# Token-major projection blocks as quads of 512-column passes

## The reference

```python
h = rms_norm(x, norm1_w[layer])
(q, k_c, v_c, k_s, v_s, k_w, v_w, g_nsa, z, xbc, dt_raw,
 gate_a, gate_b) = split_columns(h @ w_in[layer], IN_SIZES)
y_a = nsa_mixer(q, k_c, v_c, k_s, v_s, k_w, v_w, g_nsa, ...)   # 4 groups of 4 heads
y_b = ssd_mixer(z, xbc, dt_raw, ...)                           # 4 groups of 8 heads
merged = jax.nn.sigmoid(gate_a) * (y_a @ w_proj_a[layer]) + jax.nn.sigmoid(gate_b) * (y_b @ w_proj_b[layer])
x = x + merged @ w_out[layer]
x = x + conv_glu_ffn(rms_norm(x, norm2_w[layer]), ...)
```

## Time and profile before

| | |
|---|---|
| runs (median, lowest, highest) | 1243.16, 1242.79, 1243.5 us |
| span of the profiled execution | 1241.6 us |
| its own time outside the span | not given; the median lies 1.56 us above the span |
| TensorE busy in the span | 1229.4 us |
| VectorE busy | 843.6 us |
| ScalarE busy | 635.3 us |
| group stage | about 110 to 655 us, some 136.5 us for a group |

### The profile page before, as it was taken

How to read it: one execution, slowest core, us unless ns; L and a number is a source line. 1 busy time by engine, 2 the same in 40 slices (tenths; PEclk the granted TensorE clock), 3 DMA queues, 4 the chain that set the end, 5 groups by cost and what they waited for, 6 DMA issues and landing times.

```text
span 1241.6 us, 17772 instructions
## 1 busy us (share of the span) xinstructions
PE 1229.4 (99%) x6725; PEld 1054.2 (85%) x6725; DVE 843.6 (68%) x1611; ACT 635.3 (51%) x1201; POOL 88.3 (7%) x78
## 2 busy tenths in 40 slices
PE   7999999999999999999999999999999999999998
PEld 6998998899978998888978888888888888888887
DVE  4526988898879887899774643333788888884221
ACT  6616777678775868676775633223423222332110
POOL 1000001400042001400040000000000000000000
PEclk9999999999999999999999999999999999999999
DMA  8512321132212221132116623335233333334341
GB/s 243 162 34 66 86 60 47 48 105 63 63 44 74 80 67 54 51 102 61 54 40 219 222 86 93 93 97 179 64 102 96 91 102 102 88 101 136 102 128 42
DMA packets 185737, 116.34 MB, mean 94 GB/s; under 512 B 25933, under 2 KB 169909, under 8 KB 185653
## 3 DMA queue, kind: packets, MB, share of 16 engines
q1 hardware_dynamic: 182023, 108.86, 30.5%
q10 hardware_dynamic: 3630, 6.35, 1.4%
HBM read 106.80 MB, written 8.39 MB: 93 GB/s over the span
## 4 chain that ended last, share of the span: by engine, by line
PE 94%; DVE 3%; ACT 1%; issue 1%; ACTq 0%; DVEq 0%
PE g L609 16%; PE g L611 16%; PE g L610 16%; PE t L602 5%; PE g L650 5%; PE g L652 5%; PE g L651 5%; PE ob L800 3%; PE s L784 3%; PE s L959 2%; PE s L960 2%; PE s L958 2%; PE t L706 1%; PE s L881 1%; PE g L959 1%; PE g L958 1%
## 5 line engine op out<-in xcount | busy, mean ns | idle before, releaser
L1027 ACT ACTIVATE w_high<-wraw 128x1024 fp32r<-128x1024 f32 x175 | 185.2, 1059 | 279.6 <-DMA wraw<-in_ffn_w_up 135.6
L1551 DVE TENSOR_TENSOR w_low<-wraw,w_high 128x1024 fp32r<-128x1024 f32 x174 | 216.7, 1248 | 125.7 <-ACT w_high L1027 123.2
L609 PE MATMUL g<-hT_hi,w_high 128*128 128x512 f32 x360 | 158.3, 440 | 1.2 <-DVE hT_lo L1557 1.2
L650 PE MATMUL g<-w_high,hT_hi 128*128 128x256 f32 x512 | 151.7, 296 | 0.2 <-DVE w_low L1551 0.2
L652 PE MATMUL g<-w_high,hT_lo 128*128 128x256 f32 x512 | 144.7, 283 | 0.0
L651 PE MATMUL g<-w_low,hT_hi 128*128 128x256 f32 x512 | 144.6, 282 | 0.0
L611 PE MATMUL g<-hT_hi,w_low 128*128 128x512 f32 x360 | 141.1, 392 | 0.0
L610 PE MATMUL g<-hT_lo,w_high 128*128 128x512 f32 x360 | 140.9, 391 | 0.0
L609 PE MATMUL g<-h2T_hi,w_high 128*128 128x512 f32 x352 | 137.4, 390 | 0.1
L610 PE MATMUL g<-h2T_lo,w_high 128*128 128x512 f32 x352 | 137.0, 389 | 0.0
L611 PE MATMUL g<-h2T_hi,w_low 128*128 128x512 f32 x352 | 137.0, 389 | 0.0
(11 more groups left out here) (348 smaller groups left out, 2528.4 us busy)
## 6 DMA issues: line engine op xcount, KB each, us to landing
wraw<-in_w_in SPq DMA_DIRECT2D x152, 256.0 KB, 3.3
wraw<-in_ffn_w_up SPq DMA_DIRECT2D x88, 256.0 KB, 3.3
wraw<-in_ffn_w_down SPq DMA_DIRECT2D x44, 256.0 KB, 3.3
wraw<-in_w_proj_b SPq DMA_DIRECT2D x32, 256.0 KB, 3.2
yT_lo<-spill SPq DMA_DIRECT2D x6, 1024.0 KB, 10.4
spill<-piece_e ACTq DMA_DIRECT2D x16, 256.0 KB, 4.4
wraw<-in_w_proj_a SPq DMA_DIRECT2D x16, 256.0 KB, 3.2
wraw<-in_w_out SPq DMA_DIRECT2D x16, 256.0 KB, 3.3
```

What stands on the lines that cost most here:

```text
L609: nc.tensor.matmul(gb[par][:, :], w, hi, start=k == 0, stop=False)
L650: nc.tensor.matmul(out_, hT[0][:, k, cols], w, start=k == 0, stop=False)
L1027: nc.scalar.activation(whi[slot_of(u)][:, :, :], wraw[u % 2][:, :, :], ACT.Copy).then_inc(w_hi, 1)
L1551: V.tensor_tensor(wlo[slot_of(u)][:, :, :], wraw[u % 2][:, :, :], whi[slot_of(u)][:, :, :].bitcast(F32), ALU.subtract).then_inc(w_lo, 1)
```

## The change

The 28 token-major blocks become seven *quads* of four blocks: one for q, k, v in each of the first three groups, one for z in each of the four. A unit of a quad is no longer 1024 rows by 128 columns but 256 rows (two row tiles) by 512 columns; the four units q = 0 to 3 together are the 1024x512 weight. A block is the 128x512 result of one token tile i. Window n of a quad runs four of the sixteen pairs (i, q), two passes of 512 columns deep: 24 passes. Windows 0 and 1 fill the banks of tiles 0 and 1, windows 2 and 3 those of tiles 2 and 3; a tile is finished in its second window. Both windows of a half use both banks. In the second window of a quad the order is (0,2), (1,2), (0,3), (1,3); in the others a tile's two pairs follow each other. A window waits for a unit's low part only where tile 0 first uses it.

Around it: the raw loads of q, k, v have runs of 1 KB and 256 B where they had 512 B or 256 B; slots of a quad's units 0 and 1 come free in its third window, those of units 2 and 3 at its end; ScalarE copies tiles out in odd windows only, the first of the two after `exps` and ahead of `pT_hi` of tile 2; the `hi` calls stand at the ends of the iterations by a table; the C block is copied out ahead of the last y tile in groups 1 to 3; VectorE's `lo` in iterations 2 and 6 moves behind the convolution, so just ahead of `scale` of the next one.

```diff
+            def quad_window(u, n, between):
+                first, half = u - n, n % 2
+                a, b = (0, 1) if n < 2 else (2, 3)
+                c, d = 2 * half, 2 * half + 1
+                order = ((a, c), (b, c), (a, d), (b, d)) if n == 1 else ((a, c), (a, d), (b, c), (b, d))
+                for place, (i, q) in enumerate(order):
+                    if half == 0 and q == 0:
+                        pe.wait_ge(g_rel, first + i - 1)
+                    if i == 0:
+                        pe.wait_ge(w_lo, first + q + 1)
+                    w, wl = wide(whi[slot_of(first + q)]), wide(wlo[slot_of(first + q)])
+                    for kk in range(2):
+                        if 2 * place + kk in between:
+                            between[2 * place + kk]()
+                        h, l = (t[:, 2 * q + kk, P * i:P * (i + 1)] for t in hT)
+                        out_ = gb[(first + i) % 2][:, :]
+                        nc.tensor.matmul(out_, h, w[:, kk, :], start=q == 0 and kk == 0, stop=False)
+                        nc.tensor.matmul(out_, h, wl[:, kk, :], start=False, stop=False)
+                        ins = nc.tensor.matmul(out_, l, w[:, kk, :], start=False, stop=q == 3 and kk == 1)
+                    if q == 3:
+                        ins.then_inc(mm_done, 1)
+                    if n == 2 and i == 3:
+                        ins.then_inc(quad_rows, 1)
...
-                    if u in PAIRS or u - 1 in PAIRS:
-                        half_pair(u, n % 2, between)
+                    if n >= 4 or g < G - 1:
+                        quad_window(u, n % 4, between)
...
+                ROUND_END = {0: (3,), 2: (4, 5), 3: (6,), 4: (7,), 6: (8, 9), 7: (10,)}
...
+                def evac_heads(i):
+                    u = u0 + OQ + i
                     act.wait_ge(mm_done, u + 1)
+                    src = gb[u % 2][:, :].rearrange("p (b n) -> p b n", b=4)
+                    nc.scalar.activation(tokq[:, :, i, :], src, ACT.Copy)
+                    nc.scalar.activation(sq[:, :, i, :], src[:, 0:2, :], ACT.Square)
+                    nc.scalar.activation(sq_k[:, :, i, :], src[:, 2:4, 0:DH], ACT.Square).then_inc(g_rel, 1)
...
                         if 0 < n < 7 and j == 1:
                             exps(n + 1, (3, 2))
                         if n == 0 and j == 1:
-                            evac_x(g, 5)
+                            if g:
+                                hi(u0 + OQ + 2)
+                            else:
+                                evac_x(g, 5)
+                        if n % 2 and j == 1:
+                            evac_tile(n, 0)
...
-                    evac_mid(n)
+                    if n < 4 and g == G - 1:
+                        evac_block(n)
+                    elif n % 2:
+                        evac_tile(n, 1)
+                    for q in ROUND_END.get(n, ()):
+                        hi(u0 + OQ + q)
...
-                    lo(u0 + 4 + n)
+                    if n not in (2, 6):
+                        lo(u0 + 4 + n)
...
                     if n > 1:
                         conv(g, CONVS[n - 2])
+                    if n in (2, 6):
+                        lo(u0 + 4 + n)
```

More of the change, by code:

```diff
@@ L72, with last_in_slot, loads_to, blocks_done @@
 X0_UNITS = (7, 10, 11, 12)
-PAIRS = {5, 8} | {U_GRP + GROUP_BLOCKS * g + o for g in range(G) for o in ((OQ, OQ + 2, OZ, OZ + 2) if g < G - 1 else (OZ, OZ + 2))}
+PAIRS = {5, 8}
+QUADS = [U_GRP + GROUP_BLOCKS * g + o for g in range(G) for o in (OQ, OZ) if g < G - 1 or o == OZ]
 def slot_of(u):
     return (u if u < PRE_BLOCKS else u + 1) % SLOTS
-def done_for_slot(u):
+def last_in_slot(u):
     before = [v for v in range(u) if slot_of(v) == slot_of(u)]
-    if not before:
-        return 0
-    return before[-1] + (2 if before[-1] in PAIRS else 1)
+    return before[-1] if before else None
+def loads_to(u):
+    heads = [first + q for first in QUADS if (first - U_GRP) % GROUP_BLOCKS == OQ for q in range(4)]
+    return sum(48 if v in heads else 32 for v in range(u % 2, u + 1, 2))
+def blocks_done(v):
+    for first in QUADS:
+        if first + 2 <= v < first + 4:
+            return first + 4
+    return v + (2 if v in PAIRS else 1)
+def quad_rows_over(v):
+    for k, first in enumerate(QUADS):
+        if first <= v < first + 2:
+            return 2 * k + v - first + 1
+    return 0
 class Count:
@@ L424, in qkv, with wide_load, heads_rows, z_rows @@
                 sides(u, w_in_cols(g * DH + k, DH), DH, w_in_cols(g * DH + v, DH), DH)
+            def wide_load(u, w, kq, h):
+                v = w[2 * P * kq:2 * P * (kq + 1), D // 2 * h:D // 2 * (h + 1)].rearrange("(k p) n -> p k n", p=P)
+                load(u, [(wide(wraw[u % 2])[:, kk, :], v[:, kk, :]) for kk in range(2)])
+            def heads_rows(u, g, q):
+                rows = slice(2 * P * q, 2 * P * (q + 1))
+                dst = wide(wraw[u % 2])
+                qw = io["w_in"][0, rows, C_Q + 256 * g:C_Q + 256 * (g + 1)]
+                kv = io["w_in"][0, rows, C_KS:C_KS + 4 * 256].rearrange("(k p) (s n) -> p k s n", p=P, s=4)
+                load(u, [(dst[:, :, 0:256], qw.rearrange("(k p) n -> p k n", p=P))] + [
+                    (dst[:, kk, 256:512].rearrange("p (s n) -> p s n", s=4), kv[:, kk, :, DH * g:DH * (g + 1)])
+                    for kk in range(2)])
+            def z_rows(u, g, q):
+                wide_load(u, io["w_in"][0, :, C_Z + 512 * g:C_Z + 512 * (g + 1)], q, 0)
             def x_in(u, g, q):
@@ L446, in _ @@
                     if g < G - 1:
-                        qkv(u0 + OQ + b, g + 1, b)
+                        heads_rows(u0 + OQ + b, g + 1, b)
                     else:
@@ L480, in _ @@
                     halves(m * 3 + (U_MRG + q), w[:, m * P:(m + 1) * P])
-            def wide_load(u, w, kq, h):
-                v = w[2 * P * kq:2 * P * (kq + 1), D // 2 * h:D // 2 * (h + 1)].rearrange("(k p) n -> p k n", p=P)
-                load(u, [(wide(wraw[u % 2])[:, kk, :], v[:, kk, :]) for kk in range(2)])
             def out_unit(q):
@@ L1022, in hi @@
             def hi(u):
-                if done_for_slot(u):
-                    act.wait_ge(mm_done, done_for_slot(u))
-                act.wait_ge(w_loaded[u % 2], 32 * (u // 2 + 1))
+                v = last_in_slot(u)
+                if v is not None:
+                    if quad_rows_over(v):
+                        act.wait_ge(quad_rows, quad_rows_over(v))
+                    else:
+                        act.wait_ge(mm_done, blocks_done(v))
+                act.wait_ge(w_loaded[u % 2], loads_to(u))
                 nc.scalar.activation(whi[slot_of(u)][:, :, :], wraw[u % 2][:, :, :], ACT.Copy).then_inc(w_hi, 1)
@@ L1181, in y_scale, with y_back_out @@
                     nc.scalar.activation(zs[:, c, :], zs[:, c, :], ACT.Copy, scale=rstd[:, c:c + 1]).then_inc(yn_ready, 1)
-            def y_back_out(g):
+            def y_back_out(g, before_last=None):
                 act.wait_ge(t_rel, tau_of(g + 1, K_Y))
                 for b in range(4):
+                    if b == 3 and before_last:
+                        before_last()
                     tau = tau_of(g + 1, K_Y + b)
@@ L1214, in evac_gate, with evac_z, evac_tile, evac_block @@
                     hi(u + 3)
-                def evac_z(n):
-                    u, h, half = u0 + OQ + n, n % 2, n // 2 - 2
+                def evac_heads(i):
+                    u = u0 + OQ + i
                     act.wait_ge(mm_done, u + 1)
[L1220 to L1224, removed]
+                    src = gb[u % 2][:, :].rearrange("p (b n) -> p b n", b=4)
+                    nc.scalar.activation(tokq[:, :, i, :], src, ACT.Copy)
+                    nc.scalar.activation(sq[:, :, i, :], src[:, 0:2, :], ACT.Square)
+                    nc.scalar.activation(sq_k[:, :, i, :], src[:, 2:4, 0:DH], ACT.Square).then_inc(g_rel, 1)
+                def evac_z(c):
+                    u = u0 + OZ + c
+                    act.wait_ge(mm_done, u + 1)
+                    nc.scalar.activation(zs[:, c, :], gb[u % 2][:, :], ACT.Copy).then_inc(g_rel, 1)
+                def evac_tile(n, i):
+                    if n >= 4:
+                        evac_z(2 * (n // 2 - 2) + i)
+                    elif g < G - 1:
+                        if n == 1 and i == 0:
+                            act.wait_ge(v_lo, g * 2 + 2)
+                        evac_heads(2 * (n // 2) + i)
+                def evac_block(n):
                     if n == 0:
                         act.wait_ge(v_lo, g * 2 + 2)
[L1228 to L1233, removed]
+                    u = u0 + OQ + n
+                    act.wait_ge(mm_done, u + 1)
+                    nc.scalar.activation(gate_tile(n), gb[u % 2][:, :], ACT.Copy).then_inc(g_rel, 1)
                 def evac_late(q):
```

8 lines of the change are left out of this document (5 added, 3 removed).

## The result

The changed kernel takes 1247.75 us (median of 5 runs, 1247.24 to 1248.54) against 1243.17 us before (1242.79 to 1243.5), a ratio of 1.0036 with a 95% interval of 1.0023 to 1.0049. Forecast were 1246.4 us, slower, with an own range of 1244.5 to 1249.5. The span of the profiled execution grew from 1241.6 to 1246.8 us; that execution took 1248.54 us and was the slowest of the five, 0.8 us above the median, so the trace shows a little more than the 4.6 us between the medians.

The account below looks back on a forecast made before the run. TensorE was taken as the bound, with VectorE close to it. Window 1's 3.7, window 3's 2.4 and window 5's 0.4 less 3.3 saved by passes gave +3.2 us, 1246.4 us by median, range 1244.5 to 1249.5.

Parts of the forecast that it names:

- the two links of window 1: TensorE waits for a late low part at step 4, then for ScalarE's copy ahead of `cs`; 3.7 us in all.
- the signs I had named: Passes at 0.227 to 0.232 us, gaps in windows 1 and 3, group 1's z quad half a microsecond shorter.
- What the new passes save: Wide passes in quad windows: 0.15 us a window, counted for 22 windows, 3.3 us.
- Window 1: Late low part at step 4, then late `cs` transposes: +1.3, +1.3, +1.1 us in groups 0 to 2, 3.7 in all.
- the second link: ScalarE copies tile 0 out ahead of `pT_hi` of tile 2, so `cs` transposes start 1.3 us late in group 1.
- Block C's copy: C copied ahead of the last y tile holds up one transpose, up to 0.4 us in groups 1 and 2.
- Window 3: The moved low part delays `p_low(3)` and tile 2's transposes: 0.6 us in each of four groups, 2.4 us.
- Window 5: Step 4 waits for offset 9's low part: 0.1 us in each of four groups, 0.4 us.
- Behind the groups: After the group stage TensorE issues without other work to wait for, so nothing takes the shift back.
- A late head load: Rival: a quad's second head unit lands late, so TensorE waits; +8.5 us, 1251.7 us, chance 0.07.

Follow-up runs that it names:

- eight: The changed kernel with each pass of 512 columns split into two of 256; 1250.20 us.
- one: The changed kernel, but in windows 1 and 5 ScalarE copies token tile 0 out behind the high part of probability tile 3; 1245.56 us.
- two: The changed kernel, but in iterations 1 and 5 VectorE makes the low part ahead of `ttr`, not behind it; 1245.00 us.
- five: The changed kernel with the edits of one and two together; 1242.98 us.
- four: The changed kernel, but in groups 1 to 3 block C is copied out where it was before the change, behind window 0's high parts; 1247.01 us.
- nine: The kernel of six with VectorE's sum over the keys' squares moved from iteration 5 to iteration 7; 1240.04 us.
- three: The changed kernel, but in iteration 3 VectorE makes offset 7's low part between probability tiles 1 and 2, not ahead of tile 0; 1246.87 us.
- six: The changed kernel with the edits of one, two and four, and VectorE's low parts spread in iterations 3 and 4; 1241.23 us.
- ten: The kernel of nine with tiles 0 and 1 in turn in the z quad's first window, and offset 7's low part behind `scale(4)`; 1239.99 us.
- eleven: The kernel of nine with each pass of 512 columns split into two of 256; 1242.53 us.

## Why the prediction was right, point by point

The forecast was +3.2 us, measured are +4.6, and the direction, the places and the two links of window 1 were those of the traces. Passes in the quad windows start 0.231 us apart, and group 1's z quad is 0.4 us shorter than before (304.80 to 340.39, where it was 301.73 to 337.75), as the signs I had named. The parts fit less well than the sum. By windows, over all four groups, in us (measured: changes in the starts of the scores; the last row up to 640 us; the first group starts 0.1 us sooner):

| windows | forecast | measured |
|---|---|---|
| 0 and 1 | +3.7 | +5.7 |
| 2 | -0.45 | -2.7 |
| 3 | +1.95 | +3.7 |
| 4 | -0.6 | -0.8 |
| 5 | -0.2 | +0.1 |
| 6, 7 and up to the next group | -1.2 | -1.4 |

Two costs were too low, together by 3.8 us, and a gain of 2.2 us that I had not seen offsets more than half of that. That the sum came within 1.4 us is partly luck.

**What the new passes save** was over-sized. The sum had 22 windows of 0.15 us, 3.3 us; eight shows 2.45 in the changed kernel. The size per window was fair, the count was not: I left out windows 0 and 1 as set by VectorE, but not 3, 4 and 5, which in eight are no longer than in the changed kernel. The comparison of group 3 with group 1 had the right 0.6 us for four windows, and I carried it as an average to windows of another kind. The estimate by the Trainium skill ("TensorE: Matmul & The Clock Gate", section Back-to-back issue gap) gave 0.06 us a window. The section calls this formula the one of a single matmul by itself and gives other figures for a stream of weight loads and matmuls; for 512 columns these are about 131 ns, where the traces here show 231 at the full granted clock, against 216 by the formula. Windows 2 and 3 with 0.17 to 0.21 speak against 0.06 as a size; the mean of 0.09 is nearer to it, but for another reason.

**Window 1** was right in both links, and they are shown to be separate: one and two take off 2.2 and 2.75 us, five takes off nearly their sum. The size was low. I had +1.3, +1.3 and +1.1 us at the `cs` transposes; they came 1.5, 2.0 and 1.9 us late against each group's start, 5.4 instead of 3.7 us. Some 0.4 us a group is in the second link: ScalarE began to copy at 280.92, 0.77 us after the start of the pass that ends tile 0 (280.15), where I had 0.39. The three copies then took 0.92 us, as forecast. In group 1 the low part itself ended 0.15 us later than by my steps (277.61 + 1.22 = 278.83, where 277.64 + 1.04 = 278.68), and in group 2 0.5 us later (417.11, where 414.22 + 2.36 = 416.58). C's copy held up `pT_hi` and with it VectorE: in four, step 4 comes 0.17 and 0.33 us sooner after the start of groups 1 and 2.

**Block C's copy** I named, with up to 0.4 us, and then counted as nothing, since window 1 would be pinned anyway. In group 3 nothing pins it, so it costs its 0.5 us there. Four gives 0.7 us back in all: a term that was missing.

**Window 3** was right in mechanism and place: `scale(3)` and `p_low(3)` late by the moved low part, the transposes of tile 2 behind. The size was low again. The sum had 0.6 us a group; against window 3 of nine, which has none of these waits (9.2 us), the changed kernel takes 0.96 to 0.98 us more in groups 0 to 2 and 1.38 in group 3, 4.3 instead of 2.4 us. In group 1, 0.58 us of it is the wait ahead of the second transposes (300.85 to 301.66, less a pass of 0.23) and 0.2 us more time of these transposes themselves. The remaining 0.2 us is at the first transposes, and in group 3 that part is 0.6: "`scale(3)` itself is ready in time" was wrong, and it is the `piece_b` entry in the view of waits.

**A gain that I missed** is window 2. With its `lo` moved behind the convolution, `p_low(2)` follows `ttr(3)` directly and is ready 1.1 us sooner within the window (290.21, in a window that starts 3.01 us later, where it was 288.33). Before, TensorE had half a microsecond too much at the second transposes of window 2; after, nothing. First before, then the changed kernel:

```profile
288.73 0.28 PE L652 MATMUL g<-w_high,hT_lo 128*128 128x256 f32 x1
289.15 0.70 PE L602 MATMUL t<-ident,piece_b 128*128 128x128 f32 x3
```

```profile
291.48 0.40 PE L707 MATMUL g<-w_high,hT_lo 128*128 128x512 f32 x1
291.71 0.49 PE L635 MATMUL t<-ident,piece_b 128*128 128x128 f32 x3
```

The window is 0.58 to 0.71 us shorter than before in each group, 2.7 us in all where I had 0.45 from the passes. The move costs in window 3 and gives in window 2; I priced only the first side.

**Window 5** is as long as before in groups 0 to 2, where I had 0.05 us less a group. The wait for the low part at step 4 is there (0.15 us from start to start) and the saving is gone, but two shows that this wait was not what held the window: without it, the second transposes wait instead.

**Behind the groups** the profiled execution has 0.6 us more that starts after the shift of 4.6 us at the end of the group stage. It shows as short waits for low parts in the up projection, and the chain there runs through a load of 5.35 us at 980.78; the change touches none of it. The medians differ by the 4.6 us alone, and the profiles of one and three have no such wait, so I take the 0.6 us for the spread of this one execution; no run tests it.

**A late head load** did not come about: no wait of TensorE points to a load, the one wait of ScalarE for a load that the trace has in the group stage is 0.27 us, and five, six, nine and ten run with the new loads and end at or below the kernel before.

## What to carry to other kernels

When an operand is cut another way, look up for each piece when its consumer first needs it and where its producer stands in the queue: here the whole loss was the order of two engines' queues, and moving a handful of calls on ScalarE and VectorE turned 0.36% slower into 0.27% faster (1240.04 against 1243.42 us). Of these 3.4 us the passes are worth 2.5 (nine against eleven). Whether the kernel before would gain by the same reordering was not tried; it had half a microsecond of waiting in each window 2. A saving per pass counts only in the stretches that this engine sets, so count it window by window. A moved instruction has two prices, at the place it leaves and at the one it comes to.

## What the runs showed of the hardware

Two matmuls of 256 columns and one of 512 cost nearly the same: 0.12 us each and 0.227 to 0.232 us from start to start, though the profile shows 0.28 and 0.39 us for one. Joining them saved 0.17 to 0.21 us in a window with 24 of the wide ones (windows 2 and 3, nine against eleven), not the 4 us that durations suggest. What I had not expected is the delay from the last pass of an accumulation to the engine that reads it: ScalarE started 0.37 us after the end that the profile gives (280.15 + 0.40; such ends are modelled, not measured), when it had nothing else to do.
